# A hybrid scan, attention and mixture-of-experts layer on one Trainium2 core: the stages ahead of the expert loop in another order

## What is computed

```
h = rms_norm(x, norm_mix_g);  z, xbc, dt, q, k, v = split(h @ w_in)       # 1024 x 4112
y  = ssd_scan(silu(causal_conv(xbc)), softplus(dt + bias), ...)           # 16 heads of 64, state 128
y  = rms_norm per group of 512 (y * silu(z)) * ssm_norm_g
o  = rms_norm(band_attention(q, k, v, table)) * att_norm_g                # 8 heads of 64
x += concat(y, o) @ w_out                                                 # 1536 x 1024
h2 = rms_norm(x, norm_ffn_g); gates = softmax(top 4 of (h2 @ w_router + b))
x += sum over the chosen 4 of 32 experts: swiglu(h2 @ w_gate_up[e]) @ w_down[e] * gate
return rms_norm(x, norm_final_g), new keys, values, conv rows and states
```

## Time and profile before

| | us |
|---|---|
| median of 3 runs (1388.8 to 1392.68) | 1389.0 |
| the profiled execution | 1393.12 |
| its span, first to last instruction | 1391.4 |
| TensorE busy (matmuls) | 1293.1 |
| VectorE, ScalarE, GpSimd busy | 492.5, 248.7, 32.7 |
| mean granted TensorE clock | 0.966 |
| HBM traffic | 436 MB, 313 GB/s |

### The profile page before, as it was taken

One profiled execution on the slowest core, in us unless ns is written; L12 is line 12 of the kernel. 1 busy time (PEld: TensorE's weight loads), 2 busy tenths in 40 slices (PEclk: granted clock), 3 DMA queues, 4 the chain that ended last, 5 costly groups with the idle time before them and its releaser, 6 DMA issues.

```text
span 1391.4 us, 17079 instructions
## 1 busy us (share of the span) xinstructions
PE 1293.1 (93%) x6440; PEld 556.6 (40%) x6441; DVE 492.5 (35%) x950; ACT 248.7 (18%) x438; POOL 32.7 (2%) x54
## 2 busy tenths in 40 slices
PE   5998997897699999999999999999999999999995
PEld 4664654445333333333333333333333333333332
DVE  3510538434433334233333423333233232333234
ACT  2112325241111111111111111111111111111112
POOL 1000100112100000000000000000000000000000
PEclk9999998597699999999999999999999999999998
DMA  8533130110699956699599999999999996999994
GB/s 301 214 121 121 40 124 12 50 49 31 280 411 429 429 221 265 277 425 383 239 417 427 429 429 427 428 430 429 428 429 429 427 418 264 421 429 428 429 429 171
DMA packets 44633, 436.31 MB, mean 314 GB/s; under 512 B 6870, under 2 KB 7998, under 8 KB 20039
## 3 DMA queue, kind: packets, MB, share of 16 engines
q1 hardware_dynamic: 38288, 428.36, 73.6%
q0 software_dynamic: 1840, 5.81, 1.3%
q10 hardware_dynamic: 4486, 1.90, 0.5%
HBM read 432.33 MB, written 3.72 MB: 313 GB/s over the span
## 4 chain that ended last, share of the span: by engine, by line
PE 68%; DMA 23%; DVE 4%; ACT 3%; issue 1%; ACTq 1%; POOL 0%; DVEq 0%; SPq 0%; POOLq 0%
PE PS L1352 27%; DMA ring<-in_w_gate_up_dram 23%; PE PS L1387 12%; PE PS L1015 6%; PE PS L1024 5%; PE PS L1319 4%; PE PS L973 4%; PE PS L1292 4%; PE PS L1026 2%; PE PS L1341 1%; PE PS L1144 1%; ACTq L403 1%; DVE r L805 0%; PE PS L1246 0%; ACT ring L512 0%
## 5 line engine op out<-in xcount | busy, mean ns | idle before, releaser
L1352 PE MATMUL PS<-ring,r 128*64 128x512 f32 x2304 | 527.4, 597 | 22.8 <-DMA ring<-in_w_gate_up_dram 21.5
L1352 PEld LDWEIGHTS PS<-ring,r 128*64 128x64 f32 x2304 | 156.0, 136 | 319.4 <-issue 269.4
L1387 PE MATMUL PS<-ring,r 128*64 128x512 f32 x1152 | 255.1, 595 | 0.0
L912 DVE SCALAR_TENSOR_TENSOR r<-PS,gprev,r 128x512 f32<-128x512 f32 (+1 forms) x222 | 155.9, 743 | 223.6 <-PE PS L1319 223.6
L1387 PEld LDWEIGHTS PS<-ring,r 128*64 128x64 f32 x1152 | 82.2, 137 | 148.1 <-issue 148.1
L952 DVE TENSOR_TENSOR yy<-PS,yy 128x512 fp32r<-128x512 f32 x36 | 24.9, 692 | 253.1 <-ACT yy L582 253.1
L573 ACT ACTIVATE r<-r 128x512 f32<-128x512 f32 x36 | 22.7, 630 | 494.1 <-DVE r L938 494.1
L973 PE MATMUL PS<-ident,r 128*128 128x128 f32 (+4 forms) x481 | 83.2, 309 | 28.7 <-DMA e<-in_cache_v_dram 12.0
L1015 PE MATMUL PS<-r,ring 128*128 128x323 f32 x320 | 87.5, 435 | 0.0
L973 PEld LDWEIGHTS PS<-ident,r 128*128 128x128 f32 (+4 forms) x481 | 65.2, 192 | 55.1 <-issue 23.4
L1319 PE MATMUL PS<-yy,place 64*128 64x512 f32 x444 | 82.4, 449 | 4.5 <-DVE r L912 3.0
(11 more groups left out here) (261 smaller groups left out, 771.9 us busy)
## 6 DMA issues: line engine op xcount, KB each, us to landing
ring<-in_w_gate_up_dram SPq DMA_DIRECT2D x128, 2048.0 KB, 18.1
ring<-in_w_down_dram SPq DMA_DIRECT2D x64, 2048.0 KB, 18.1
ring<-in_w_in_dram SPq DMA_DIRECT2D x8, 2048.0 KB, 11.6
ring<-in_w_out_dram SPq DMA_DIRECT2D x3, 2048.0 KB, 7.5
r<-in_x_prompt_dram SPq DMA_DIRECT2D x2, 512.0 KB, 3.8
r<-bias_table_clipped ACTq DMA_DIRECT2D x4, 256.0 KB, 8.9
out_dram<-r POOLq DMA_DIRECT2D x2, 512.0 KB, 4.1
r<-in_x_prompt_dram POOLq DMA_DIRECT2D x2, 512.0 KB, 3.5
```

The costliest lines, as they stand in the source:

```text
L912: v.scalar_tensor_tensor(xx, PS[0:rows, 6 + h, :], gprev[0:rows, t:t + 1], xx, ALU.mult, ALU.add)\
L1352: last = mm(PS[64 * h:64 * h + 64, m, :], xt[:, k % 4, k // 4, :], w[:, kk, D * m + 512 * h:D * m + 512 * h + 512], start=False, stop=(k = ...
L1387: last = mm(PS[64 * h:64 * h + 64, 2, :], at[:, kk, c, :], w[:, kk, 512 * h:512 * h + 512], start=(c == 0 and kk == 0), stop=(c == 1 and k ...
```

## The change

The front gets another order; the expert loop and what follows it stay as they are.

- The small loads fall into groups: seven gains and the conv history ahead of the first squares, five `head` loads after them, four (`late`: cached keys and values, router weights) and the initial state from GpSimd's queue. Each tile of x has its own semaphore, and SyncE asks for the weight chunks without waiting.
- The chunks of w_in come in the order conv channels, z, q, k, v. The dt product gives rows at once. ScalarE applies the silu as it empties z from PSUM.
- q, k and v are computed beside the scan, through a "lane" of two PSUM banks (7 and 1) that also takes the transposes of the mixed rows, the states and the keys; `lane_mm` and `lane_ev` count its twenty uses.
- w_out is applied in parts: `ssd_part` (four matmuls for one group of a long tile, eight for the sample) and `att_part` (four). Each part goes to a bank, nearly always bank 7, and VectorE adds it to x with the norm factor as a scalar (`add_part`), so that the long tiles are not scaled before. The six steps of attention stand between the SSD parts.
- The router takes the unnormalised rows of x, turned by `turn_rows`; its weights carry the gain, and the row factor is applied to the logits (`route`). The normalised rows for the experts are made after that, and ScalarE's part of their splitting (`token_parts`) stands for all three tiles behind its last eviction of turned rows.

```diff
-W_IN_CHUNKS = [C_XBC, C_XBC + 512, C_XBC + 1024, C_Q, C_Q + 512, C_Q + 1024, C_Z, C_Z + 512]
+W_IN_CHUNKS = [C_XBC, C_XBC + 512, C_XBC + 1024, C_Z, C_Z + 512, C_Q, C_Q + 512, C_Q + 1024]
...
-                if i < 6:
-                    sp.wait_ge(s["proj_mm"], 4 * i + 4 if i < 5 else 21 + NT)
+                if i < 3:
+                    sp.wait_ge(s["proj_mm"], 4 * i + 4)
+                elif i < 5:
+                    sp.wait_ge(s["proj_mm"], 12 + NT * (i - 2))
                 elif i < N_IN:
-                    sp.wait_ge(s["z_mm"], NT * (i - 5))
+                    sp.wait_ge(s["lane_mm"], (LANE_Q, LANE_K, LANE_V)[i - 5])
+                elif i < N_IN + 2:
+                    sp.wait_ge(s["out_mm"], SSD_PARTS)
                 else:
-                    sp.wait_ge(s["out_mm"], 2 * NT)
+                    sp.wait_ge(s["out_mm"], OUT_PARTS)
...
-            sp.wait_ge(s["x_in"], 48)
-            sp.wait_ge(s["small_in"], N_SMALL * 16)
...
+            def residual(t):
+                pool.wait_ge(s["sqrt2"], t + 1)
+                if t < 2:
+                    pool.wait_ge(s["lane_mm"], LANE_MIX[t])
+                else:
+                    pool.wait_ge(s["turn_mm"], 1)
...
+            segments_exp(5)
+            values_out(2)
+            for q in range(2):
+                state_rows(0, q, lane()).then_inc(s["lane_ev"], 1)
+            act.wait_ge(s["y_mm"], 5)
+            for q in range(4):
+                act.dma_start(bias[:, 2 * q:2 * q + 2, :], bass.AP(
+                    table_d, head_of(q // 2, 2 * (q % 2)) * 383, [[1, 128], [2 * 383, 2], [1, 256]]))\
+                    .then_inc(s["bias_in"], 16)
+            norm_ssd(1)
+            mixed_out(1, 0)
+            mixed_out(1, 1)
+            for t in range(NT):
+                keys_out(t)
...
+            mean_square(0)
+            half_turned(0)
+            attended_out(2)
+            mean_square(1)
+            half_turned(1)
+            mean_square(2)
+            half_turned(2)
+            for t in range(NT):
+                token_parts(t)
             act.wait_ge(s["rexp"], 1)
             a.activation(pv[:, :, :], pv[:, :, :], ACT.Exp).then_inc(s["pv_ready"], 1)
...
+            def add_ssd(n):
+
+                t, h, gg = (n // 4, n // 2 % 2, n % 2) if n < 8 else (2, n - 8, 0)
+                if n % 4 == 0:
+                    dve.wait_ge(xres_in[t], 16)
+                dve.wait_ge(s["out_mm"], n + 1)
+                if n:
+                    dve.wait_ge(s["out_ev"], n)
+                add_part(t, h, 7, 0, stat[:, 12 + 3 * t + gg:13 + 3 * t + gg])
...
+            def add_part(t, h, b, at, scale):
+                if t < 2:
+                    xx = x[:, t, 512 * h:512 * h + 512]
+                    last = v.scalar_tensor_tensor(xx, bank(b), scale, xx, ALU.mult, ALU.add)
...
+            def route(t):
+                rows = ROWS[t]
                 dve.wait_ge(s["sqrt3"], t + 1)
                 step(v.reciprocal(stat[0:rows, 6 + t:7 + t], stat[0:rows, 3 + t:4 + t]))
+                dve.wait_ge(s["lgt_mm"], t + 1)
+                step(v.scalar_tensor_tensor(lg[0:rows, t, :], PS[0:rows, (1, 7, 1)[t], 32 * t:32 * t + 32], stat[0:rows, 6 + t:7 + t],
+                                            brt[0:rows, :], ALU.mult, ALU.add))
...
+            chunk_outputs(3)
+            value_lane(wv, 1)
+            segment_sums(5)
+            value_lane(wv, 2)
+            state_lane(0)
+            state_lane(1)
+            chunk_outputs(4)
+            mixed_lane(1, 0)
+            mixed_lane(1, 1)
+            key_lane(0)
+            key_lane(1)
+            chunk_outputs(5)
+            key_lane(2)
+
...
+            def ssd_part(n):
+
+                t, h, gg = (n // 4, n // 2 % 2, n % 2) if n < 8 else (2, n - 8, 0)
+                if n % 4 == 0:
+                    if t < 2:
+                        pe.wait_ge(s["lane_ev"], LANE_MIX[t])
+                    else:
+                        pe.wait_ge(s["mixS_ready"], 1)
+                if n < 2:
+                    pe.wait_ge(w_full[slot_of(N_IN + n)], front_arrival(N_IN + n))
+                if n:
+                    pe.wait_ge(s["out_ev"], n)
+                groups = (gg,) if t < 2 else (0, 1)
+                for j in groups:
...
+                        last = rows_by(7, t, mixS[:, 4 * j + c, TCOL[t]:TCOL[t] + ROWS[t]],
+                                       w_out_rows(j)[:, c, 512 * h:512 * h + 512],
+                                       j == groups[0] and c == 0, j == groups[-1] and c == 3)
+                last.then_inc(s["out_mm"], 1)
...
+            scores(2)
+            ssd_part(4)
+            turn_weights(1)
+            ssd_part(5)
+            weigh_values(1)
...
+            weigh_values(5)
+            pe.wait_ge(s["mx_ready"], 6)
+            att_part(3)
+            turn_rows(0)
+            pe.wait_ge(s["out_ev"], 13)
+            turn_attended(2)
             logits(0)
-            project(2, 0)
+            turn_rows(1)
+            att_part(4)
+            att_part(5)
             logits(1)
-            project(2, 1)
+            turn_rows(2)
             logits(2)
```

More of the change, by code:

```diff
@@ new lines, in _ @@
+            dve.wait_ge(s["bias_in"], 64)
+            step(v.memset(bias[0:64, :, 0:64], NEG))
+            softmax(0)
+            add_ssd(0)
+            add_ssd(1)
+            add_ssd(2)
+            weights_turned(0)
+            softmax(1)
+            dve.wait_ge(s["sqrt2"], 3)
+            v.reciprocal(stat[0:SS, 18:20], stat[0:SS, 18:20]).then_inc(s["rec2"], 1)
+            add_ssd(3)
+            attended(0)
+            add_ssd(4)
+            weights_turned(1)
+            softmax(2)
@@ new lines, in _ @@
+            add_ssd(5)
+            attended(1)
+            add_ssd(6)
+            weights_turned(2)
+            softmax(3)
+            add_ssd(7)
+            attended(2)
+            bias_parts(0)
+            add_ssd(8)
+            weights_turned(3)
+            softmax(4)
+            dve.wait_ge(s["sqrt5"], 1)
+            step(v.reciprocal(stat[:, 14:15], stat[:, 14:15]))
+            add_ssd(9)
+            attended(3)
+            add_att(0)
+            weights_turned(4)
+            softmax(5)
@@ L1066, in _ @@
                     pe.wait_ge(s["t2_dve"], 3 * t)
[L1067 removed]
                 for q in range(2):
[L1069 to L1071 removed]
+                    last = tr(PS[0:rows, 4, 64 + 128 * q:64 + 128 * q + 128], conv[:, XT + q, hc])
                 last.then_inc(s["t2_mm"], 1)
+            w = chunk(4)
```

972 lines of the change are left out of this document (551 added, 421 removed).

## The result

The changed kernel takes **1374.41 us** (median of four runs, 1373.22 to 1376.27); the kernel before, run beside it, 1390.55. The ratio is 0.9882, with a 95% interval of 0.9864 to 0.9900: faster by 1.2%. The forecast was 1370.0 with a range of 1361 to 1381.

A forecast was written before the change was run, and what follows sets the result against it. The expert loop's 1018.3 us were taken as fixed, so an earlier front ends the kernel equally earlier. Six steps put the loop at 354.1, 19.0 earlier: 1393.1 - 19.0 = 1374.1, by the median 1370.0 us; range 1361 to 1381.

The forecast's parts named there:

- Step 1: Start, up to the first projections: regrouped loads and tile-by-tile norms let them begin at 17.0 us, a gain of 5.2.
- Step 2: Projections before the scan, with step sizes, z and transposes: 102.7 us, so the scan stage starts at 119.7.
- Step 3: Scan beside q, k, v: 100.1 us, with 5.4 idle, 2.0 of small waits and 3.6 of lower clock; end at 219.8.
- Step 4: Attention beside the SSD rows of the projection: 71.8 us of TensorE work plus 5.6 for handoffs; end at 297.2.
- Step 5: From there to the last transposed rows: 15.6 us with waits plus 3.7 of slow-down; ScalarE free at 316.5.
- Step 6: The tail: splitting delays the exponent, choice over experts starts 17.8 us later, at 334.3; loop 19.86 behind it, at 354.1.
- A: Better: clock stays up at scan's end and in step 5, start as early as 15; 1360 to 1361 us, chance 0.07.
- B: Slower than before: clock falls at scan's end and stays at half through step 4, up to 1442 us; chance 0.04.
- C: Same as before: unfound holes hold up sixteen products by 1 to 2 us each; 1385 to 1391 us, chance 0.03.
- D: Holding up of products as in C but only partly, a hidden 10 to 15 us: 1380 to 1385 us, chance 0.09.

The follow-up runs named there:

- run 7: Changed kernel with SyncE issuing the weight chunks only after x and the parameters have arrived: 1381.25 us, ratio 0.9932.
- run 3: Changed kernel with the four bias loads issued from SyncE's queue instead of ScalarE's: 1366.16 us, ratio 0.9815.
- run 6: Changed kernel with all q, k and v groups ahead of the scan instead of between its matmuls: 1387.08 us, ratio 0.9981.
- run 1: Changed kernel with the exponent of the routing weights ahead of the splitting of all three tiles on ScalarE: 1365.69 us, ratio 0.982.
- run 2: Changed kernel with tile 0's splitting moved ahead of the last tile's mean square, exponent still last: 1370.53 us, ratio 0.9866.
- run 4: Changed kernel with twelve unused matmuls filling TensorE's hole ahead of the key rows at the scan's end: 1370.32 us, ratio 0.9853.
- run 5: Changed kernel with the bias data in eight loads of one head instead of four of two, still on ScalarE: 1377.78 us, ratio 0.9902.
- run 8: Changed kernel with bias loads on SyncE's queue, tile 0's splitting earlier and the exponent between tile 1's two copies: 1352.89 us, ratio 0.9734.
- run 10: Kernel of run 8 with GpSimd's subtractions in four pieces of 256 columns: 1355.2 us, ratio 0.9735.
- run 9: Kernel of run 1 with GpSimd's subtractions in four pieces of 256 columns: 1368.02 us, ratio 0.9824.

## Why the prediction was right

**What bounds the kernel.** Right: the loop's length changed by 0.4 us, the rhythm not at all, and every run that moved the loop's start moved the end by about as much. The forecast had the loop at 354.1; it starts at 355.7. The other 3 us between 1370.0 and 1374.4 come from the step from profile to median. I took off 4.1, because the profiled run of before lay that far above the median of three; the changed kernel's profiled run lies 0.95 above its median, and the kernel before has medians of 1390.0 to 1391.6 in the larger samples. It was a difference of samples, not of the profile.

**Step 1** (start 17.0, measured 18.45): I argued by parameters and norms and took off 1 for the chunk. The rows were turned at 17.8 and the chunk came 0.65 us behind them; run 7 shows that without the chunk's early request the start gains nothing (24.54 against 22.20 before the change). That I had one of two nearly equal limits and not the other cost little, which is luck.

**Step 2** (102.7, measured 103.8): the groups took 54.2 instead of 52.4 and the first half of z 16.0 instead of 14.0 in a stage with a clock of 0.95, where I had counted full clock. The second part follows a term that the sum priced rightly and looked at no further, the step sizes. Before they were

```profile
109.60 4.53 PE L1039 MATMUL PS<-r,wdt 128*16 128x323 f32 x16
```

and now they and the long tiles of z are

```profile
73.84 5.88 PE L1231 MATMUL PS<-wdt,r 128*128 128x16 f32 x48
79.65 16.01 PE L1195 MATMUL PS<-ring,r 128*128 128x512 f32 x32
```

Sixteen instructions with 323 columns left the clock at 1.00 before. Now 48 with 16 columns take their place, and the clock is 0.61 and 0.53 in the two windows from 76 to 84 us, though TensorE is busy throughout. It falls about there in all eleven profiles of the new order, those of the runs included. The two rows together took 18.5 us before and 19.9 in the sum, and take 20.4 to 22.0 in these profiles. No run tried the old form, so the link is argued from these rows.

**Step 3** (100.1, measured 100.45): the hole was named with its cause and its clock. Its size was off: 6.71 instead of 5.4, because the four issues took 3.48 us and not the 1.99 of the earlier trace rows. Run 3 shows that hole and clock were worth 8.5 us at the loop's start (9.7 counted from the v rows, 8.3 in the medians); the sum had 9.0. Run 6 shows that the rest of the step, the cover for VectorE's 41 us, is where most of the change's gain lies.

**Step 4** (77.4, measured 80.3): the handoffs were as small as I said, the waits in the rows being 0.2 to 0.9. What was missing is lower clock: one product at 5.28, one at 5.40, 1.6 and 1.7 more than 3.70. That a hole goes on costing in the stage behind it was in step 3's sum for 3.6 us and not in step 4's; what slowed the product of 5.40 is open.

**Step 5** (19.3, measured 16.3) was too dear: the first logits ran at full clock (1.94), and only the last two products were slow (5.04 instead of 3.67).

**Step 6** (17.8 to the choice, measured 17.4; 19.9 from there, measured 19.1) was right in mechanism and size, and runs 1 and 2 confirm it: take the splitting away from ahead of the exponent and the wait of 12.5 us goes, or 5.6 of it for one tile. On the table load: it took 1.28, and the exponent follows 0.01 us behind its end, as the trace shows (335.00 and 336.29). The drain of about 1.4 us that the Trainium skill, "ScalarE: Activation LUTs", section "What ACT_TABLE_LOAD costs", adds to a switch is not seen here.

**The rivals.** A (clock stays up) didn't come; run 4 shows what its half at the scan's end was worth, 3.6 us. That this is the forecast's figure is partly luck, since 1.9 of it come at the scan's end and 1.7 at the product of 291.88. B fell with run 5 and with the clock of 0.95 in step 4. The Trainium skill, "TensorE: Matmul & The Clock Gate", section "A second HAM failure mode: psum-queue depth-cycling", describes gaps that let the clock oscillate; here gaps of 0.2 to 0.9 us between products left it at 1.00 from 228 to 292 and one of 0.62 was followed by a product at half clock (291.88), which cost 1.7 us where B needed 19. The same gap of 0.62 was followed by full clock in runs 3, 4, 6, 8 and 10, so the trace doesn't show that the gap lowers it. C and D supposed holes that I had not found: the sum of the six steps was off by 1.6 us in all. The first four steps were too cheap by 5.8 us together and the last two too dear by 4.2, and that they nearly cancel is luck.

## What to carry to other kernels

An order that puts one engine's long work beside another's chain gains what was bare before (here 12.7 us in the medians for ten groups of matmuls in the scan), and gives it back wherever a short step stands behind long ones in some queue. So read each queue of the new order for small instructions that others wait for: the exponent of 0.21 us behind 16 us of splitting, and the squares behind four DMA issues, cost 21.5 us together in a change that gained 16. When runs are compared by one profile each, count from a point just ahead of the edit: here the unedited stretch before it differed by up to 4.6 us. A hole on TensorE is to be priced twice, as time and as the slower work behind it, and the second part falls into the next stage's sum.

## What was unexpected in the hardware

- **The same four DMA issues took 3.48 us on ScalarE's queue** beside the scan, 1.99 at the start of the kernel before and 1.96 in run 6; on SyncE's queue in run 3 they took 2.47. The load of the DMA engines doesn't explain it: their busy share was 0.97 during the 3.48, 1.05 during the 1.99 and 0.37 during the 1.96. The cause stays open.
- **GpSimd holds VectorE.** In run 1, VectorE operations of 0.16 to 0.22 us (elementwise operations, a cast, a copy, a scan) took up to 2.12 and ended with GpSimd's subtraction beside them, while reductions kept their length; with pieces of a quarter the holds fell to 0.4 to 0.7. The Trainium skill, "SBUF — State Buffer", section "Who interferes with whom", has this as a port pair that whoever starts first keeps for its whole instruction, and says that reductions don't take part. The trace agrees in both. It asks for care when a tail's GpSimd work is moved beside a chain of small VectorE operations.
- **Filling a hole with useless matmuls gained 3.6 us** at the loop's start, though the key rows just behind the hole start no earlier (run 4).
- One product (291.88) ran at half clock in the changed kernel and in runs 1, 2, 5, 7 and 9, and at full clock in runs 3, 4, 6, 8 and 10, behind the same wait of 0.62 us. The loop's start has 1.7 us of it. The hole of the scan's end was closed or filled in 3, 4, 8 and 10, but not in run 6, so the cause stays open.
- **The clock fell on a TensorE without a gap**, with or just behind the 48 narrow matmuls of the step sizes, in every profile of the new order (step 2). A busy share of 1 in the profile did not mean full clock.
